# Rounding streamed weights on GpSimd: a copy instruction written as a multiply by one

## The reference

```python
# each layer of the second block
h = layer_norm(ALPHA * h + y, ln_g[i, 0], ln_b[i, 0])
u = jnp.square(jax.nn.relu(h @ w_up[i])) @ w_down[i]          # 1024 -> 4096 -> 1024
h = layer_norm(ALPHA * h + u, ln_g[i, 1], ln_b[i, 1])
h = h + jax.nn.sigmoid(h @ w_ple_gate[i]) * (p[i] @ w_ple[i])
# inside differential attention, for every head pair
a = jax.nn.softmax(s, axis=-1).reshape(B, H, 2, BLOCK, ke)
a = a[:, :, 0] - lam_full * a[:, :, 1]
```

## Time and profile before

| | us |
|---|---|
| median of 3 executions | 4570.45 |
| lowest and highest | 4555.87 and 4571.16 |
| the profiled execution's own time | 4571.16 |
| its span in the profile | 4569.4 |
| TensorE busy | 3884.2 (85%) |
| DVE busy | 2151.7 (47%) |
| GpSimd busy | 1906.2 (42%) |
| ACT busy | 913.8 (20%) |

### The profile page before, as it was taken

The page is one execution under the profiler, slowest core; times in us unless marked ns, Lnnn a source line. Parts: engine busy times, 40 slices in busy tenths (PEclk is TensorE's granted clock), DMA queues, the critical chain, the costliest instruction groups (busy, mean ns, idle before and its releaser), DMA issues. The chain is left out here.

```text
span 4569.4 us, 50243 instructions
## 1 busy us (share of the span) xinstructions
PE 3884.2 (85%) x18060; PEld 3130.4 (69%) x18060; DVE 2151.7 (47%) x2855; ACT 913.8 (20%) x2199; POOL 1906.2 (42%) x687
## 2 busy tenths in 40 slices
PE   8999987656689769998976599988889988859998
PEld 6877764445567558886865488866678876747886
DVE  2232335784345645544346455433454535645553
ACT  2333331100212311101033111014411112311111
POOL 5443412310144136564543356642155643235563
PEclk9999986775589879998987799988899999979999
DMA  3228821245222112222210122221122222112221
GB/s 125 94 84 103 100 46 42 95 126 106 73 85 74 56 56 92 100 93 74 100 39 0 46 98 95 92 75 62 43 83 101 92 80 92 65 46 83 101 92 69
DMA packets 105235, 363.23 MB, mean 79 GB/s; under 512 B 25014, under 2 KB 51894, under 8 KB 69512
## 3 DMA queue, kind: packets, MB, share of 16 engines
q1 hardware_dynamic: 83376, 331.97, 24.3%
q10 hardware_dynamic: 21720, 29.37, 2.1%
HBM read 335.17 MB, written 30.34 MB: 80 GB/s over the span
## 5 line engine op out<-in xcount | busy, mean ns | idle before, releaser
L293 POOL CAST wh<-raw 128x2048 fp32r<-128x2048 f32 x269 | 511.1, 1900 | 2227.3 <-PE bank L335 1506.5
L295 POOL TENSOR_TENSOR wl<-raw,wh 128x2048 fp32r<-128x2048 f32 x269 | 1263.1, 4696 | 21.5
L333 PE MATMUL bank<-XTh,wh 128*128 128x512 f32 x2320 | 927.5, 400 | 68.8 <-DVE XTl L2639 44.1
L334 PE MATMUL bank<-XTh,wl 128*128 128x512 f32 x2320 | 914.0, 394 | 0.0
L335 PE MATMUL bank<-XTl,wh 128*128 128x512 f32 x2320 | 913.3, 394 | 0.0
L333 PEld LDWEIGHTS bank<-XTh,wh 128*128 128x128 f32 x2320 | 442.7, 191 | 187.0 <-issue 89.2
L335 PEld LDWEIGHTS bank<-XTl,wh 128*128 128x128 f32 x2320 | 441.8, 190 | 94.7
L334 PEld LDWEIGHTS bank<-XTh,wl 128*128 128x128 f32 x2320 | 442.7, 191 | 89.4
L333 PE MATMUL bank<-wh,XTh 128*128 128x512 f32 (+2 forms) x1056 | 394.7, 374 | 49.2 <-PEq L509 26.0
L333 PE MATMUL bank<-wh,HTh 128*128 128x512 f32 x1024 | 404.5, 395 | 0.0
L334 PE MATMUL bank<-wh,HTl 128*128 128x512 f32 x1024 | 404.5, 395 | 0.0
(11 more groups left out here) (320 smaller groups left out, 4844.4 us busy)
## 6 DMA issues: line engine op xcount, KB each, us to landing
raw<-in_weights SPq DMA_DIRECT2D x270, 1024.0 KB, 4.8
MO<-ssm_out SPq DMA_DIRECT2D x8, 1024.0 KB, 4.8
B<-bias_d ACTq DMA_DIRECT2D x8, 1024.0 KB, 5.5
B<-bias_a ACTq DMA_DIRECT2D x8, 512.0 KB, 7.1
bias_d<-tab SPq DMA_DIRECT2D x16, 256.0 KB, 13.9
ssm_out<-CA SPq DMA_DIRECT2D x16, 256.0 KB, 2.6
ssm_in<-W2T SPq DMA_DIRECT2D x8, 512.0 KB, 2.7
ssm_out<-lag_kernel SPq DMA_DIRECT2D x16, 256.0 KB, 4.6
```

What stands on the lines that cost most here:

```text
L293: pool.tensor_copy(wh[s][:, :], raw[r][:, :]).then_inc(w_high.h, 1)
L295: pool.tensor_tensor(wl[s][:, :], raw[r][:, :], wh[s][:, :].bitcast(F32), ALU.subtract).then_inc(w_split.h, 1)
L333: nc.tensor.matmul(psum, sh, mh, start=first, stop=False)
L334: nc.tensor.matmul(psum, sl, mh, start=False, stop=False)
```

## The change

The instruction that writes the high part of a weight chunk was a copy with a change of type. It is now a multiplication by the constant 1.0 with the same input and the same output, at both places where weights are split:

```diff
@@ split_chunk (L293)
             pool.sem_inc(split_ready.h, 1)
-            pool.tensor_copy(wh[s][:, :], raw[r][:, :]).then_inc(w_high.h, 1)
+            pool.tensor_scalar(wh[s][:, :], raw[r][:, :], 1.0, None, ALU.mult).then_inc(w_high.h, 1)
             pool.wait_ge(w_high.h, c + 1)
@@ split_high (L300)
             pool.wait_ge(raw_in[k].h, 16)
-            pool.tensor_copy(wh[k][:, :], raw[k][:, :]).then_inc(w_high.h, 1)
+            pool.tensor_scalar(wh[k][:, :], raw[k][:, :], 1.0, None, ALU.mult).then_inc(w_high.h, 1)
```

## The result

The changed kernel took 4683.9 us in the median (4674.98 to 4693.53 over four timed runs) against 4570.8 us before (the median of four executions now): a ratio of 1.0253, 95% interval 1.022 to 1.0287. The forecast was 4573 us, same, and its range ended at 4627: wrong, on the slower side.

The account below looks back on a forecast made before the run. TensorE was taken as the bound (busy 85%), with GpSimd waiting for it. Twenty places paying 0.13 us each gave +2.6 us on 4571.16, so 4573.8, forecast as 4573 us for the median; 8-in-10 range 4550 to 4627.

Parts of the forecast that it names:

- x: Duration of the new GpSimd multiplication that replaces each 1.90 us cast; forecast 2.03 us.
- d: Added time per replaced cast on GpSimd, the new duration less 1.90 us; forecast +0.13 us.
- The dearer case: Rival: multiplication takes 2.2 to 5.86 us, still hidden in steady state; +23 us at 3.05, +56 at 4.70; chance 0.25.
- From above: Upper estimate of the multiplication's duration from the two-input subtraction L295, 4.70 us: 2.8 us more per cast, +56 us total.
- The sum of 20 d: All places where the cast's added time was to be paid, 20 in number: 20 x 0.13 = +2.6 us.
- differential attention 16 d: Two differential attentions: 14 long L1111 and 2 long L1110, each delaying TensorE by the cast's added time once.
- The gate 1 d: State-space gate: first split runs beside L2635, on the chain to the first matmul; pays the added time once.
- the opening 1 d: Opening phase: L474 waits for the cast and TensorE's transposes for L474; pays the added time once.
- the late chunk 1 d: Chunk at 56.27 us whose DMA landed late, TensorE waiting for wl; pays the added time once.
- Steady chunks hidden up to x = 5.86: 172 steady chunks and most others: GpSimd's 3.96 us idle piece hides the longer high part; cost zero up to 5.86 us.
- Each microsecond more on the cast is one more for DVE: Differential attention: DVE gets free only when the whole split ends, so added cast time passes one for one to TensorE.
- The race at the cast's end: Rival in differential attention: later end signal or earlier release lets L1111 run before L295, some 25 us faster, 4546 us; chance 0.05.

Follow-up runs that it names:

- e5: Changed kernel with the two-operation form (multiplication by 1.0, addition of 0.0) on streamed chunks, first chunk by a copy: 4573.1 us, ratio 1.0006.
- e7: Kernel before with the copy done three times per streamed chunk: 4727.3 us, ratio 1.0352.
- e14: Changed kernel (one multiplication of 2048 elements) with the subtraction in four pieces: 4676.8 us, ratio 1.0237.
- e15: Changed kernel with the multiplication in two pieces and the subtraction in four: 4619.4 us, ratio 1.0124.
- e4: Kernel before with two fills of zeros into the same buffer ahead of each copy: 4643.7 us, ratio 1.0167.
- e9: Changed kernel with its multiplication in two pieces of 1024 elements, the subtraction in one: 4576.9 us, ratio 1.0032.
- e6: Kernel before with the copy done twice per streamed chunk: 4606.9 us, ratio 1.0085.
- e1: GpSimd alone, copies and arithmetic forms timed singly, no kernel around them: at 2048 elements one operation 5.37 us, two operations 1.90 us.
- e13: GpSimd and DVE alone, one split beside a dependent DVE chain: chain ends after 7.54 us beside the copy, 10.54 beside the multiplication, 2.36 beside its halves.

## Why the prediction was wrong

*The term that failed is x.* The prediction took 2.03 us, d = +0.13; it was 5.37 in the median, d = +3.47. The inference "one multiplication per element need not slow it" was wrong by 2.54 against the assumed 0.88 ns per element. The sign was in its own rows: L535 with one operation at 240 ns against L521 with two at 200. The prediction saw it, priced it at 5 ns per element more (10.2 us in all, three times the true 3.47) and gave that 0.08. Its other estimate, 3.07 us, was too low as well. The dearer case's price from L295's 4.70 us was the nearest.

*The bounds.* "From above" by L295 (d = 2.8) was too low for the range's end; 12.1 us was the only bound that held.

*The sum of 20 d.* With the true d it gives 20 x 3.47 = +69 us, 4640, still above the range's end of 4627 but 44 us short; the medians say +113, the profiled executions +124 over e5. So a second step failed beside x, the count of places, and with it the claim that TensorE's busy time stays unchanged. Term by term: differential attention 16 d = 56, measured 60, and that closeness is luck: the waits for L1112, which were to grow by 16 d, grew by 34 to 38 us, TensorE was busy 23 to 26 us longer at the lower granted clock (the first numbers against the kernel before, the others against e5), and the sequence is another than d being added once. (The trace before has 15 L1111 above 4.6 us, not 14.) The gate 1 d = 3.5 (2 to 3 measured; L2635's eight pieces took 11.7 us instead of 9.9), the opening 1 d (1.6 measured, since DVE gets free before the multiplication ends), the late chunk 1 d (TensorE's wait grew by 2.3). Not counted: the state-space preparation, 18 us; dilated attention, some 10 beyond the late chunk; feed-forward 9, where I had zero only for d under 1.8; sliding attention 11 to 13 instead of 3.5, at L1748 and not at L1232, which did not change. I had looked for DVE instructions that were long already and ended a TensorE wait; a chain of dependent DVE instructions that is itself the bound (L2284 to L2295) shows no such wait and is held just the same.

*Steady chunks hidden up to x = 5.86.* Right at x = 5.37: the idle piece is 0.6 us, and e7, e14 and e15, whose splits exceed the slack, pay 51 to 72 us in the feed-forward blocks. The limit is a little too generous: e4's split of 10.53 us in the median, 3.78 over the 6.75 before, stands for x = 5.68 and pays 25 there, e9's of 10.20 pays 4.

*"Each microsecond more on the cast is one more for DVE."* Wrong as a law. e6 and e7 lengthen the split by 2.0 and 4.0 us at +5 and 0 us in differential attention, e9 by 3.6 at -15. What DVE pays there is the length of the instruction that it runs into, and then of the next one.

*The race at the cast's end turned after all,* by the second of the rival's two conditions (GpSimd lets go of DVE earlier), but not to a gain: L1111 now runs ahead of the subtraction, and L1112 stands under it. The sign that 14 long L1111 would still be there failed with it. The rival priced L1111's release and forgot its successor, the very question that it should have asked.

## What to carry to other kernels

Time an unfamiliar form of an instruction by itself at its real size, with each operand form, before reasoning about what hides it: here one left-out operand nearly trebled it. An engine whose busy time grows without new work is being held, but how much it costs is read from the waits of the engine behind it. In a chain of dependent instructions each can meet a GpSimd instruction of its own, so what counts is the length of one times the number that the chain meets; cutting long GpSimd instructions into four or eight pieces gave 0.9% here, into two nothing, as long as the whole stays clearly under the period of the engine that it feeds. Look at TensorE's busy time too: with the same matmuls it grew by 61 us. Read an experiment by phase and not by its total: e14's total was the changed kernel's, for another reason.

## What the runs showed of the hardware that was not expected

- GpSimd's TENSOR_SCALAR with one operation: 5.37 us at 128x2048, with two 1.90; at 1024 elements 2.77 (e1).
- A two-input DVE instruction beside the one-operation form gets free before that ends: 3.64 us into 5.37, 1.05 us into 2.77 (e13). Both are some 1.7 us before the end; why is open. The Trainium skill (SBUF — State Buffer, section "Who interferes with whom") says, of DVE's two-port modes, that whoever issues first keeps the shared pair for its whole instruction: by these rows a hold lasts as long as the copy (L89) and the subtraction (L90, L91), but not as long as this form (L89). Nor does the order of the starts in the trace tell who is held: L90 starts at 10.34 us, the subtraction at 10.38, and L90 is held. Its other rule there, that a write-only GpSimd instruction does not hold a two-input DVE instruction, agrees: 0.16 us beside a fill.
- L90 took 1.96 us beside the single multiplication, 0.49 beside the half (e13). Why is open.
- Beside L2294 the multiplication itself grew from 5.37 to 5.94 us (5.74 and 5.84 us beside the feed-forward block's DVE work): GpSimd is slowed as well.
- In the two differential attentions the granted clock fell to its lower level 19 times instead of 9, and the same matmuls took 428 us instead of 405.
